# Dilated attention in one decoder layer: queries and keys laid down in the token order of each dilation

## The reference, cut to what matters

```python
DILATED_GROUPS = ((128, 1), (512, 4), (2048, 16))      # (window, dilation)
def dilated_group(q, k, v, window, dilation):
    nk = window // dilation                            # 128 keys in every group
    def to_blocks(t):   # tokens r, r + dilation, r + 2*dilation, ... form one row of blocks
        t = t.reshape(B, L, dilation, H, hd).transpose(0, 2, 3, 1, 4)
        ...
    s = jnp.einsum('brhnqe,brhnke->brhnqk', qb, kb)    # own block and the block before
    s = jnp.where(valid, s, -jnp.inf)
    ...
```

## Time and profile before

| | |
|---|---|
| median of 3 runs | 1816.27 us (1815.85 to 1816.5) |
| the profiled execution, its time | 1814.24 us |
| its span in the trace | 1812.6 us |
| TensorE busy | 1775.8 us, 98% of the span |
| TensorE weight loads busy | 1509.5 us, 83% |
| VectorE busy | 1085.6 us, 60% |
| ScalarE busy | 699.3 us, 39% |
| granted TensorE clock | full in all 40 slices |

### The profile page before, as it was taken

One profiled execution on the slowest core, in us unless ns is written; L12 is line 12 of the kernel. 1 busy time (PEld: TensorE's weight loads), 2 busy tenths in 40 slices (PEclk: granted clock), 3 DMA queues, 4 the chain that ended last, 5 costly groups with the idle time before them and its releaser, 6 DMA issues.

```text
span 1812.6 us, 26619 instructions
## 1 busy us (share of the span) xinstructions
PE 1775.8 (98%) x9186; PEld 1509.5 (83%) x9186; DVE 1085.6 (60%) x1927; ACT 699.3 (39%) x1597; POOL 479.0 (26%) x574
## 2 busy tenths in 40 slices
PE   6999999999999999999999999989999999999999
PEld 6888888988888889898978888868888888878887
DVE  5352553644636848484966545686555555566776
ACT  5333333243334353444453223553332333244443
POOL 3010001101116342332411000026565565420210
PEclk9999999999999999999999999999999999999999
DMA  7212321423122101111136323322332223288674
GB/s 210 86 43 65 95 76 65 128 64 111 58 74 79 59 24 59 35 58 29 49 124 216 105 82 105 117 77 98 110 116 93 102 101 110 83 295 303 230 231 170
DMA packets 169810, 196.38 MB, mean 108 GB/s; under 512 B 9552, under 2 KB 119472, under 8 KB 169216
## 3 DMA queue, kind: packets, MB, share of 16 engines
q1 hardware_dynamic: 157904, 165.23, 28.5%
q0 software_dynamic: 5552, 19.65, 3.3%
q10 hardware_dynamic: 6272, 10.49, 1.6%
HBM read 150.88 MB, written 44.45 MB: 108 GB/s over the span
## 4 chain that ended last, share of the span: by engine, by line
PE 77%; issue 10%; DVE 7%; POOL 4%; ACT 1%; DMA 1%; SPq 0%; POOLq 0%; ACTq 0%; DVEq 0%
PE bank L2332 18%; PE bank L2334 18%; PE bank L2333 18%; PE lvl_ps L2334 5%; PE lvl_ps L2332 5%; PE lvl_ps L2333 5%; PE bank L2420 3%; POOL dbuf L865 1%; POOL dbuf L864 1%; PE bank L2446 1%; DVE fbuf L1841 1%; PE bank L2432 1%; PE lvl_ps L2471 1%; DVE fbuf L1842 1%; PE lvl_ps L2527 1%
## 5 line engine op out<-in xcount | busy, mean ns | idle before, releaser
L2332 PE MATMUL bank<-act_hi,w_hi 128*128 128x512 f32 x568 | 227.8, 401 | 0.3 <-ACT gbuf L1094 0.3
L2334 PE MATMUL bank<-act_hi,w_lo 128*128 128x512 f32 x568 | 221.8, 391 | 0.0
L2333 PE MATMUL bank<-act_lo,w_hi 128*128 128x512 f32 x568 | 221.2, 389 | 0.0
L2332 PE MATMUL bank<-ca,wq 128*128 128x512 f32 x528 | 206.2, 391 | 7.7 <-DVE wq L2077 5.3
L2334 PE MATMUL bank<-ca,wq 128*128 128x512 f32 x528 | 205.5, 389 | 0.0
L2333 PE MATMUL bank<-ca,wq 128*128 128x512 f32 x528 | 205.5, 389 | 0.0
L2332 PE MATMUL bank<-w_hi,act_hi 128*128 128x256 f32 (+1 forms) x576 | 179.9, 312 | 3.0 <-DVE act_lo L1610 3.0
L2334 PE MATMUL bank<-w_hi,act_lo 128*128 128x256 f32 (+1 forms) x576 | 176.7, 307 | 0.0
L2333 PE MATMUL bank<-w_lo,act_hi 128*128 128x256 f32 (+1 forms) x576 | 176.6, 307 | 0.0
L2332 PEld LDWEIGHTS bank<-act_hi,w_hi 128*128 128x128 f32 x568 | 106.8, 188 | 22.9 <-issue 1.3
L2334 PEld LDWEIGHTS bank<-act_hi,w_lo 128*128 128x128 f32 x568 | 106.6, 188 | 22.9
(11 more groups left out here) (366 smaller groups left out, 4204.8 us busy)
## 6 DMA issues: line engine op xcount, KB each, us to landing
w_raw<-in_w_in SPq DMA_DIRECT2D x60, 512.0 KB, 4.2
rawd<-in_w_ffn_down SPq DMA_DIRECT2D x99, 256.0 KB, 4.9
rx<-y_scratch SPq DMA_DIRECT2D x77, 256.0 KB, 4.5
wr<-in_w_ffn_gate SPq DMA_DIRECT2D x11, 1024.0 KB, 5.4
wr<-in_w_ffn_up SPq DMA_DIRECT2D x11, 1024.0 KB, 5.4
y_scratch<-sq SPq DMA_DIRECT2D x11, 1024.0 KB, 4.3
y_scratch<-yq SPq DMA_DIRECT2D x33, 256.0 KB, 2.0
gate_scratch<-gbuf ACTq DMA_DIRECT2D x32, 256.0 KB, 2.0
```

The lines of the kernel that those rows point to most:

```text
L2332: pe.matmul(ps, lhs_hi, rhs_hi, start=first, stop=False, skip_group_check=onto)
L2333: pe.matmul(ps, lhs_hi, rhs_lo, start=False, stop=False, skip_group_check=onto)
L2334: return pe.matmul(ps, lhs_lo, rhs_hi, start=False, stop=last, skip_group_check=onto)
```

## The change

The operands of the scores of groups 1 and 2 are stored so that each unit's 128 (or 256) tokens lie side by side. For the queries, ScalarE's copy out of bank 6 is split: where a job holds the queries of groups 1 and 2, each is copied by an instruction of its own (`in_order`), which reads the bank with a step of 4 or 8 and writes runs of 16 to 64 elements. The keys are kept three times: in token order in `qk_t[:, 0]`; in the order of group 1 in `k_g1`, which lies in the `rot` buffer and is written by one ScalarE copy in pass 9, after the last evacuation; in the order of group 2 in `qk_t[:, 1]`, where group 0's query was, written by one ScalarE copy in pass 10, after group 0's scores. A new semaphore `k_order` makes TensorE wait for the first before batch 4 and for the second before batch 8. The scores then take plain slices.

```diff
+    k_g1 = rot[:, :, :, :].rearrange("p a i q -> p (a i q)")
+
+    def in_order(g, tiles):
+
+        r, tt, w = 4 * g, tiles[0], len(tiles)
+        if g == 1:
+            out = qk_t[:, 2, :].rearrange("p (r b j) -> p r b j", r=r, b=2)[:, :, tt // 4,
+                                                                          32 * (tt % 4):32 * (tt % 4) + 32 * w]
+        else:
+            out = qk_t[:, 3, :].rearrange("p (r j) -> p r j", r=r)[:, :, 16 * tt:16 * tt + 16 * w]
+        if w == 2:
+            return (out.rearrange("p r (t j) -> p r t j", t=2),
+                    banks[6].rearrange("p (t m j r) -> p r t m j", t=2, m=2, r=r)[:, :, :, g - 1, :])
+        return out, banks[6][:, P * (1 + g):P * (2 + g)].rearrange("p (j r) -> p r j", r=r)
...
-                    dst = qk_t[:, c0:c0 + n, P * tiles[0]:P * tiles[0] + P * len(tiles)]
-                    if len(tiles) == 2:
-                        act.copy(dst.rearrange("p m (t d) -> p t m d", d=P),
-                                 banks[6].rearrange("p (t m d) -> p t m d", t=2, d=P)).then_inc(t2_evac, 1)
-                    else:
-                        act.copy(dst, banks[6].rearrange("p (m d) -> p m d", d=P)).then_inc(t2_evac, 1)
+                    if c0 == 0:
+                        dst = qk_t[:, 0:2, P * tiles[0]:P * tiles[0] + P * len(tiles)]
+                        if len(tiles) == 2:
+                            mm = act.copy(dst.rearrange("p m (t d) -> p t m d", d=P),
+                                          banks[6].rearrange("p (t m d) -> p t m d", t=2, d=P))
+                        else:
+                            mm = act.copy(dst, banks[6][:, 0:2 * P].rearrange("p (m d) -> p m d", d=P))
+                    if c0 + n == 4:
+                        for g in (1, 2):
+                            mm = act.copy(*in_order(g, tiles))
+                    mm.then_inc(t2_evac, 1)
+                if s == 9:
+                    act.wait_ge(t2_evac, 8 * h + 8)
+                    act.copy(k_g1.rearrange("p (r j) -> p r j", r=4),
+                             qk_t[:, 0, :].rearrange("p (j r) -> p r j", r=4)).then_inc(k_order, 1)
...
+                if s == 10:
+                    act.wait_ge(s_ready, NB * h + 4)
+                    act.copy(qk_t[:, 1, :].rearrange("p (r j) -> p r j", r=8),
+                             qk_t[:, 0, :].rearrange("p (j r) -> p r j", r=8)).then_inc(k_order, 1)
                 for j in EXP_AT.get(s, []):
...
+                if b in (4, 8):
+                    pe.wait_ge(k_order, 2 * h + b // 4)
                 for i in range(2):
                     g, n, prev = unit(b, i)
-                    q = tokens(qk_t[:, 1 + g, :], g, n)
+                    q = qk_t[:, 1 + g, P * n:P * n + P]
                     o = score_ps[b % 2][:, 2 * P * i:2 * P * i + 2 * P]
-                    if g == 0:
-                        kk = qk_t[:, 0, P * (n - prev):P * n + P]
-                    elif g == 1:
-                        r = n // 2
-                        kk = qk_t[:, 0, r:r + (8 if prev else 4) * P - 3:4]
-                    else:
-                        kk = tokens(qk_t[:, 0, :], g, n)
+                    kk = (qk_t[:, 0, :], k_g1, qk_t[:, 1, :])[g][:, P * (n - prev):P * n + P]
                     mm = pe.matmul(o if prev else o[:, P:], q, kk, start=True, stop=True)
```

More of the change, by code:

```diff
@@ L294, in decoder_layer @@
     t2_ready, t2_evac = sem("t2_ready"), sem("t2_evac")
+    k_order = sem("k_order")
     s_ready, masked, neg_max, p_done = sem("s_ready"), sem("masked"), sem("neg_max"), sem("p_done")
@@ L458, in unit @@
         return g, n, (g == 0 and n > 0) or (g == 1 and n % 2 == 1)
-    def tokens(t, g, n):
-        if g == 0:
[L463 to L467, removed]
     def done(p, j):
```

## The result

The changed kernel takes 1796.67 us in the median of 4 runs (1796.22 to 1796.87), against 1816.06 us for the kernel before, measured beside it: a ratio of 0.9896, 95% interval 0.9884 to 0.9908. It is faster by 19.4 us. The forecast was 20.5 us less, 1795.8 us, with a range of 1793 to 1801.

What follows compares the result with a forecast made beforehand. TensorE was taken to bound phase A. Plain batches save 20.7 us, pass 13 loses 0.2, added ScalarE work costs nothing: 20.5 us off, 1793.7 from the profiled execution, 1795.8 on the median; range 1793 to 1801.

Steps and rivals of the forecast that it cites:

- TensorE's list sets the end of phase A, and the gain stays: Phase A: TensorE hardly idles, so time off its list comes off the end and stays; 20.5 us gained.
- The price of the batches: Score batches of groups 1 and 2: 9.58 us a head strided, 4.40 plain; 5.18 saved, 20.7 us in four heads.
- Either operand might carry the cost, it need not be known: Score batches: both operands become plain, so whether weight load or moving operand carries the cost was left open; no size.
- Added ScalarE work costs nothing: Split evacuations and key copies (1.03 to 2.02 us, 1.5 taken) on ScalarE are hidden; costed at nothing.
- The stall in the middle of pass 13: Pass 13, value products waiting for VectorE's u_t copy: 0.05 us lost, 0.2 us in four heads.
- the prediction's own sign of being wrong: Wrong if TensorE idles in passes 10-13 before L2432 or L2446, waits at L2420 for ScalarE, or shows long score records.
- Rival 1: Second batches of a pass give their gain back, waiting for u_t or pt copies: 11.3 us lost, 1807; 1 in 10.
- rival 2: Group 1 scores are slow for another reason than their step; only group 2 gains, 8.7 us, 1807.5; 1 in 25.
- rival 3: Score records are slow from VectorE and ScalarE running beside them, not layout; no change, 1816 us; 1 in 25.
- rival 4: ScalarE's key copy of pass 10 far dearer; from 4.4 us pass 11 waits; 1824 us at 11.5; 1 in 33.

Runs made afterwards that it cites:

- experiment 1: Two edits of the changed kernel: queries plain with keys read by step, 1813.59 us; keys plain with queries read by step, 1807.37 us.
- Experiment 4: The changed kernel with the key copy of pass 10 made three times in a row: 1809.26 us, 13.2 us above the control.
- e1: The changed kernel with queries side by side but keys of groups 1 and 2 read with a step of 4 or 8: 1813.59 us.
- e2: The changed kernel with keys side by side in three copies but queries read with a step of 4 or 8: 1807.37 us.
- e4: The changed kernel run once more, unaltered, as control on the same chip: 1796.07 us.
- e5: The changed kernel with GpSimd's two additions held back until the head's last row maxima are made, in heads 2 to 4: 1795.73 us.
- e7: The changed kernel with the key copy of pass 10 made three times in a row: 1809.26 us.
- e3: The kernel before, with group 1 read at step 2 instead of 4 and group 2 at step 3 instead of 8 (wrong tokens): 1799.27 us.
- e6: The changed kernel with VectorE's u_t copy placed before the small multiplication that makes the negated maxima: 1795.6 us.

## Why the prediction was right, and where it was off

- *TensorE's list sets the end of phase A, and the gain stays.* Right: the last statistics turn comes 18.0 us earlier (548.0 to 530.0), and the spans of the same two executions differ by 18.0 us. Nothing gave it back later.
- *The price of the batches.* Right to 0.02 us: 0.66 and 0.44 were worked out from group 0's rows and the value products, 0.65 and 0.66, 0.44 and 0.44 were measured. A head's batches fell from 9.58 to 4.38 us; the sum of 5.18 us a head measured 5.20, and the turns behind them lost their stretch too, 0.1 us a head.
- *Either operand might carry the cost, it need not be known.* Right for the time, and experiment 1 told what each is worth: plain queries alone gave 2.1 us, plain keys alone 8.4, and the rest needs both.
- *Added ScalarE work costs nothing.* Right, with the size off: the key copies take 2.06 and 2.21 us, above both ends of my 1.03 to 2.02. The split evacuations were cheap: 0.66 us for two copies. Experiment 4 shows the cover: 5.4 us for the copies of pass 10 before the first turns wait (three take 6.5 us, the turns are 1.15 late), where I had 4.4.
- *The stall in the middle of pass 13.* The step was found, and mis-sized: 0.05 us a head, against 0.10 in the first head and 0.49 in the others. By the prediction's own sign of being wrong, TensorE idle before the value products in passes 10 to 13, it was wrong at this step: there are 0.33 us of idle time in three heads. That the time lies so near the forecast all the same is because the step is small beside the batches. Besides, pass 12, where I took nothing, loses 0.08 more (281.31 to 281.64 is three turns, 0.33 us, but from 281.64 the first two products take 0.30 instead of 0.22). Of the 0.49, 0.10 comes from the 0.15 us from VectorE to TensorE, for which I had 0.06 us of slack and no price. The other 0.39 is a meeting that I did not look for: the heads are shorter, GpSimd's additions start at a fixed distance behind VectorE's product of pass 12, and now reach into pass 13. The multiplication of pass 13 starts 6.82 us after that product before the change (297.64 - 290.82) and 6.32 after it (289.24 - 282.92): it came 0.50 nearer, what batch 10's scores lost. Before, it met only the last 0.12 us of the addition (which ended at 297.76) and took 0.17 us.
- The account: a head gains 5.3 us by its batches and turns and loses 0.57 in heads 2 to 4 (0.49 and 0.08) and 0.18 in the first: 3 x (5.3 - 0.57) + (5.3 - 0.18) = 19.3 us, against 19.4 measured. Rival 1 was the true direction of the small miss, at 0.6 us a head instead of its full 2.8.
- Rivals 2, 3 and 4 fell by the rows of the changed kernel: group 1 gained most, the slow records are gone, and the copy took 2.21 us, under the 4.4 from which rival 4 counts. Experiment 4 adds that this rival's price was too low: some 1.2 us too much of copies cost 3.3 us a head, since one late list meets TensorE three times.

One number needs a caution. The profiled execution of before is the fastest of its runs, 1814.24 us, and has a granted clock of 1.00 from 20 to 40 us; that of the changed kernel has 0.91 there, and its first scores start at 120.3 us instead of 118.9. Five of the other traces have the same 0.91 (`e1`, `e2`, `e4`, `e5`, `e7`); `e3` and `e6` have 1.00, and `e6`, a changed kernel too, starts its first scores 1.5 us before the control. So it goes with the execution, not with the change. Span against span (1812.6 to 1794.6) therefore shows only 18.0 us; the medians and the head lengths show the change.

## What to carry to other kernels

A distance between starts, taken where the operand is plain and where it is strided, priced this change to 0.02 us a batch; the recorded lengths of pipelined matmuls could not. Lay down both operands of a matmul in order, or at a step of at most two fp32 elements: one side alone gave 2 (the stationary one) and 8 (the moving one) of the 19 us. When the bound engine gets faster, look for every instruction of the other engines that keeps its distance to something else, for it will now lie beside another neighbour; here a 2-column multiplication on VectorE met a GpSimd addition, and the price was paid by TensorE.

## What the runs showed of the hardware

- A float32 matmul whose moving operand is read with a step of 4 or 8 elements streams at half rate: 0.91 us for 4 x 128 columns and 1.34 for 2 x 128 and 2 x 256, against 0.44 and 0.65. With both operands strided, step 2 is nearly free (0.69 us for 0.65) and step 3 costs half as much (0.69 for 0.44).
- A weight load of 128 columns with a step of 4 or 8 takes 308 to 341 ns, and four of them with plain keys set a batch of 0.83 to 1.04 us, 0.21 to 0.26 each; plain ones take some 190 ns, and four 128-column matmuls with them take 0.44 us.
- ScalarE too pays for a step in SBUF: 2.06 us for 1024 columns read with a step of 4, 2.21 with 8, against 1.03 for a plain cast of that size (no run has a plain copy). Its copies out of PSUM with a step of 4 or 8 showed no such price (0.66 us for two of 256 columns, 0.59 for one plain of 512).
- A VectorE multiplication of two columns took 0.64 us instead of 0.17 beside a GpSimd addition and ended 0.02 us after it; a copy out of PSUM in the same place took its usual 0.42.
- From the end of a VectorE copy to the start of the matmul that waits for it pass 0.15 us (three kernels).
